# Modulation rows of a DiT layer: two alternating accumulators, one product with ones per step, plain stores, biases added behind

## The reference, cut to what matters

```python
mod_x = (jax.nn.silu(c) @ w_mod[l] + b_mod[l])[:, None, :]        # 1024 -> 6 * 1024
mod_c = (jax.nn.silu(c_ctx) @ w_mod[l] + b_mod[l])[None, None, :]
sh1, sc1, g1, sh2, sc2, g2 = jnp.split(mod_x, N_MOD, axis=-1)
...
hx = modulate(x, norm_mix_g[l], sh1, sc1)      # rms_norm(x) * (1 + scale) + shift
hc = modulate(ctx, norm_mix_g[l], csh1, csc1)
fx, qx, kx, vx = split_projection(hx @ w_in[l])     # 1024 -> 1536
fc, qc, kc, vc = split_projection(hc @ w_in[l])
...                                             # q, k normed per head, rotary; attention; Fourier mix
x = x + g1 * (jnp.concatenate([four_x, attn_x], axis=-1) @ w_out[l])
x = x + g2 * expert_choice_ffn(modulate(x, norm_ffn_g[l], sh2, sc2), ...)   # 16 experts
```

## Time and profile before

| | |
|---|---|
| median of 3 runs | 2109.92 us (2108.83 to 2115.02) |
| profiled execution, its own time | 2115.79 us |
| its span, first to last instruction | 2114.0 us |
| TensorE busy | 1878.2 us, 89% |
| DVE busy | 1604.0 us, 76% |
| ACT busy | 1305.0 us, 62% |
| POOL busy | 267.5 us, 13% |
| mean granted TensorE clock | 0.95 |

### The profile page before, as it was taken

The page is one execution under the profiler, slowest core; times in us unless marked ns, Lnnn a source line. Parts: engine busy times, 40 slices in busy tenths (PEclk is TensorE's granted clock), DMA queues, the critical chain, the costliest instruction groups (busy, mean ns, idle before and its releaser), DMA issues.

```text
span 2114.0 us, 28075 instructions
## 1 busy us (share of the span) xinstructions
PE 1878.2 (89%) x8737; PEld 1469.3 (70%) x8737; DVE 1604.0 (76%) x2017; ACT 1305.0 (62%) x1930; POOL 267.5 (13%) x303
## 2 busy tenths in 40 slices
PE   6889758988998998843999999999999999999993
PEld 2667545666666666623888888888888888888882
DVE  1576745686767667637988989998988889998983
ACT  2634215675667656622777777777777777777772
POOL 0133211121111111100111001100111001100111
PEclk9989878999999999976999999999999999999996
DMA  8255437021011101024999999999999999999985
GB/s 340 87 138 155 119 85 183 19 61 60 20 40 60 42 27 50 30 110 154 413 392 378 380 400 388 376 381 388 401 378 384 374 401 385 377 375 392 393 314 196
DMA packets 103747, 509.69 MB, mean 241 GB/s; under 512 B 12504, under 2 KB 36496, under 8 KB 53008
## 3 DMA queue, kind: packets, MB, share of 16 engines
q1 hardware_dynamic: 95264, 482.55, 60.4%
q0 software_dynamic: 5120, 16.80, 3.3%
q10 hardware_dynamic: 3312, 9.70, 1.2%
HBM read 479.11 MB, written 27.30 MB: 240 GB/s over the span
## 4 chain that ended last, share of the span: by engine, by line
PE 50%; issue 2%; DVE 2%; DMA 1%; ACT 0%; POOL 0%; ACTq 0%; POOLq 0%; SPq 0%
PE banks L1476 32%; PE banks L1501 16%; PE banks L1488 1%; PE banks L1457 1%; DVE topi L1347 1%; DVE top L1345 1%; DVE cand L1348 1%; DMA xe<-h_scratch,icol 0%; DMA acc_scratch<-ysc,idx_s 0%; DVE raw L1440 0%; ACT raw L1334 0%; DMA raw<-acc_scratch 0%; POOL fst L1261 0%; POOL fst L1263 0%; POOL gate_s L1244 0%
## 5 line engine op out<-in xcount | busy, mean ns | idle before, releaser
L1379 DVE TENSOR_TENSOR w_lo<-raw,w_hi 128x2048 fp32r<-128x2048 f32 x256 | 574.6, 2285 | 67.8 <-ACT w_hi L1283 67.8
L1283 ACT ACTIVATE w_hi<-raw 128x2048 fp32r<-128x2048 f32 x256 | 470.5, 1919 | 8.5 <-DMA raw<-in_w_exp 8.5
L1476 PE MATMUL banks<-w_hi,x_hi 128*128 128x512 f32 x1024 | 405.5, 396 | 1.4 <-DVE x_lo L1373 1.4
L1476 PE MATMUL banks<-w_hi,x_lo 128*128 128x512 f32 x1024 | 400.1, 391 | 0.0
L1476 PE MATMUL banks<-w_lo,x_hi 128*128 128x512 f32 x1024 | 399.5, 390 | 0.0
L1387 DVE TENSOR_TENSOR d_lo<-raw,d_hi 128x1024 fp32r<-128x1024 f32 x256 | 296.1, 1216 | 1.5 <-ACT d_hi L1305 1.4
L1305 ACT ACTIVATE d_hi<-raw 128x1024 fp32r<-128x1024 f32 x256 | 258.3, 1061 | 35.8 <-DMA raw<-in_w_exp 21.1
L1476 PEld LDWEIGHTS banks<-w_hi,x_lo 128*128 128x128 f32 x1024 | 192.7, 188 | 40.8
L1476 PEld LDWEIGHTS banks<-w_hi,x_hi 128*128 128x128 f32 x1024 | 193.0, 189 | 39.8 <-DVE x_lo L1373 1.8
L1476 PEld LDWEIGHTS banks<-w_lo,x_hi 128*128 128x128 f32 x1024 | 193.1, 189 | 38.2
L977 DVE TENSOR_TENSOR ptl<-banks,pth 128x384 fp32r<-128x384 f32 x320 | 176.3, 554 | 55.7 <-ACT pth L923 51.4
(11 more groups left out here) (195 smaller groups left out, 2781.8 us busy)
## 6 DMA issues: line engine op xcount, KB each, us to landing
raw<-in_w_exp SPq DMA_DIRECT2D x384, 1024.0 KB, 7.8
a_ring<-in_w_mod SPq DMA_DIRECT2D x32, 512.0 KB, 4.4
qt<-q_scratch SPq DMA_DIRECT2D x64, 192.0 KB, 3.5
a_slot<-in_w_mod SPq DMA_DIRECT2D x8, 1024.0 KB, 13.7
a_w_raw<-in_w_in SPq DMA_DIRECT2D x3, 2048.0 KB, 27.5
q_scratch<-a_qst SPq DMA_DIRECT2D x16, 384.0 KB, 3.9
a_xt<-in_x ACTq DMA_DIRECT2D x8, 512.0 KB, 3.7
xr<-in_x SPq DMA_DIRECT2D x8, 512.0 KB, 4.2
```

What stands on the lines that cost most here:

```text
L1283: act.activation(w_hi[which][c][:, :], raw[which][c][:, :], ACT.Copy).then_inc(s["hi_done"], 1)
L1379: dve.tensor_tensor(w_lo[which][c][:, :], raw[which][c][:, :], w_hi[which][c][:, :].bitcast(F32), ALU.subtract).then_inc(s["lo_done"], 1)
L1476: i = pe.matmul(psum[:, 2 * (j % 2) + which, :], x_[par][:, k, :], w_, start=(k == 0 and w_ is hi and x_ is x_hi), stop=(k == KD - 1 and x ...
```

## The change

1. The accumulator is one tile of 128 x 2 x 256. A step's two units advance together: DVE's instructions alternate between the two halves of the tile, first the lower halves of both units (`modulation(n, 0)`, ahead of `sums`), then the upper halves (`modulation(n, 1)`, between `sums` and `rotate`). Each waits for the one before it on its own half, thus two back, in place of a wait after each instruction. Nothing stands between `rotate` and `low` any more.
2. One product with ones per step, of 512 columns, behind `project(n, 2)`. ACT copies it to a row `mrow` of its own ahead of the next `normal`; SP stores it plainly ahead of `store`. POOL has no DMA left in phase A. The accumulator is free when the product has been made (`row_mm`).
3. The ring's order: a step's four halves are now (unit 0 low, unit 1 low), (unit 0 high, unit 1 high).
4. The biases are added in phase B: SP loads four more vectors of `b_mod` (512 KB each as spread) behind `rows` and ahead of `x2`, and POOL adds them in four instructions of 128 x 1024 ahead of the two that make `rows[SC2]`.
5. Prologue: ACT rounds chunk 2 of `w_in` only behind the last `c_rows` copy; tile 1 of x is loaded earlier; chunks 1 and 0 are rounded at other places; the square of a tile is written to PSUM, not to SBUF. `ON_DVE` is empty, so all of the first eight units stay on TensorE and `first_unit` is not called.

```diff
-            sp.dma_start(mod_d, a["b_mod"][0][2 * D:6 * D]).then_inc(s["preset"], 16)
...
+            def row_store(n):
+                sp.wait_ge(s["row_ev"], n + 1)
+                sp.dma_start(mod_d[n * 2 * UM:(n + 1) * 2 * UM].unsqueeze(0), mrow[:, :]).then_inc(s["row_out"], 16)
...
-                for i in range(2 * units[0], 2 * units[0] + 3) if units else ():
-                    load(i)
+                for i in range(3) if TC <= n < TS else ():
+                    load(4 * (n - TC) + i)
+                if TC < n <= TS:
+                    row_store(n - 1 - TC)
                 if n >= 2:
                     store(n - 2)
-                if units:
-                    load(2 * units[0] + 3)
+                if TC <= n < TS:
+                    load(4 * (n - TC) + 3)
...
-            def row_out(u):
...
-                pool.dma_start(mod_d[u * UM:(u + 1) * UM].unsqueeze(0), acc[u % 2][0:1, :], accum_op=ALU.add).then_inc(row_out_done[u % 2], 16)
...
-                if u >= NC_UNITS - 2:
-                    weights(2, u - NC_UNITS + 2)
+                if i == 1:
+                    load_x(1)
+            weights(2, 0)
+            weights(2, 1)
...
+            def modulation(n, half):
+                i0 = 4 * n + 2 * half
+                last = [(s["mod_used"], i0 - 1), (s["mod_used"], i0)] if half else [None, None]
                 if half == 0:
-                    after(dve, row_out_done[u % 2], 16 * (u // 2))
+                    after(dve, s["row_mm"], n)
                 for k in range(4):
+                    for x in range(2):
+                        slot_ = (i0 + x) % RING
+                        if k == 0:
+                            dve.wait_ge(ring_in[slot_], 16 * ((i0 + x) // RING + 1))
+                        ins = weigh(acc[:, x, :], ring[slot_][:, k * UM:(k + 1) * UM], c_sig[:, 4 * half + k, 0:1], last[x], half == 0 and k == 0)
...
-                pe.matmul(psum[0:1, MB, 0:UM], ones[:, 0:1], acc[u % 2][:, :], start=True, stop=True).then_inc(s["row_mm"], 1)
+                pe.matmul(psum[0:1, MB, :], ones[:, 0:1], acc[:, :, :].rearrange("p a n -> p (a n)"), start=True, stop=True).then_inc(s["row_mm"], 1)
...
-            sp.dma_start(x2[:, :], a["norm_ffn_g"][0].partition_broadcast(P)).then_inc(s["rows_in"], 16)
+            for dst, v in ((h2[:, :], a["b_mod"][0][2 * D:3 * D]), (junk2[:, :], a["b_mod"][0][3 * D:4 * D]), (h2t[:, :, :].rearrange("p k n -> p (k n)"), a["b_mod"][0][4 * D:5 * D]),
+                           (xr[:, :], a["b_mod"][0][5 * D:6 * D]), (x2[:, :], a["norm_ffn_g"][0])):
+                sp.dma_start(dst, v.partition_broadcast(P)).then_inc(s["rows_in"], 16)
...
-            pool.wait_ge(s["rows_in"], 32)
+            pool.wait_ge(s["rows_in"], 16 * 6)
+            for i, tmp in ((G1, h2[:, :]), (SH2, junk2[:, :]), (SC2, h2t[:, :, :].rearrange("p k n -> p (k n)")), (G2, xr[:, :])):
+                pool.tensor_tensor(rows[:, i, :], rows[:, i, :], tmp, ALU.add).then_inc(s["bias_done"], 1)
```

More of the change, by code:

```diff
@@ L203, in w_parts @@
         return 2 * (2, 1, 0).index(c)
-    def units_of(n):
-        return (2 * (n - TC), 2 * (n - TC) + 1) if lat(n) else ()
+    ON_DVE = ()
+    ON_PE = tuple(u for u in range(NC_UNITS) if u not in ON_DVE)
     with nc.Block() as block:
@@ new lines, in first_unit @@
+            def first_unit(i, u):
+                last = [None, None]
+                dve.wait_ge(unit_in[u], 16)
+                for k in range(KD):
+                    for j in range(2):
+                        ins = weigh(first_acc[i][:, j, :], slot[u][:, k, :], c_sig[:, k, j:j + 1], last[j], k == 0)
+                        if k == KD - 1 and j == 1:
+                            ins.then_inc(s["first_used"], 1)
+                        else:
+                            order[0] += 1
+                            ins.then_inc(s["dve_order"], 1)
+                            last[j] = (s["dve_order"], order[0])
```

180 lines of the change are left out of this document (93 added, 87 removed).

## The result

The changed kernel takes 2095.7 us (median of 4 runs, 2094.6 to 2099.4) against 2111.2 us (2108.8 to 2115.0) of the kernel before, run beside it: 15.5 us less, ratio 0.9928, 95% interval 0.9908 to 0.9948. Measured a second time beside later experiments it was 2095.4 us, ratio 0.9932 (0.9911 to 0.9952). The forecast was 16.5 us less.

The account below looks back on a forecast made before the run. DVE's chain of work and waits was taken to bound the latent steps, TensorE following. Phase A -28.5 and phase B +12 make -16.5 us, forecast 2093 us; the range leaving out 2 in 10 is 2083 to 2107.

Parts of the forecast that it names:

- The wait: Phase A: DVE's wait for the accumulating DMA, 42.7 us in 7 waits, holds up the latent steps and would go.
- The step, 20.7 us: Latent step's DVE chain: ring landed 11.6, seven instructions 2.8, rotary 4.98, `low` 1.27; 20.7 us against 25.6 before.
- The clock in the steps: Latent steps: TensorE's wait stays under a microsecond, so its clock holds.
- TensorE alone, 20.0 us: Phase A step if only TensorE bound it: 17.8 us, plus one wide product and the transposes of `queries`.
- The alternation, 0.40 an instruction: DVE's modulation: an alternating instruction takes 0.40 us, where linked ones take 0.51; at 0.51, 4 us of gain go.
- The prologue, +2.0: Before the first projection: chunk 2's second rounding starts 1.9 us later, and the first projection with it, +2.0 us.
- Phase A, -28.5 in all: Step 9 begins at 223.5 against 252.04, so phase A takes 28.5 us less.
- Phase B, +12: Start of phase B: transfer 7.9 and additions 9.6 against 6.7 of slack, plus 1.2 of slow clock: +12 us.
- The lock: Rival, phase A: POOL's square starts before `low`, each step 1.7 us longer, about 13 us in all, 2106; chance 0.17.
- slower mechanism: Rival, phase A: ring load late, each microsecond beyond 4.4 going into some 6 steps; chance 0.12, half of it above 2104.
- The kernel with hidden biases: Rival: loads land at 3.5 us and phase B loses only 6, 9 us better, 2084; chance 0.10.
- A landing at 8.5 us: Case of a late ring load in phase A: at 8.5 us the kernel is 7 us slower, 2118.

Follow-up runs that it names:

- experiment 4: Kernel before the change with four accumulators and four DMA semaphores in place of two, ACT's square written to PSUM: 2082.8 us, 0.9872.
- three edits and queries: Changed kernel with fourth ring half loaded between stores, chunk 2's roundings earlier, biases added inside tile 0, ACT's queries ahead of normalization: 2074.7 us, 0.9836.
- four accumulators and queries: Kernel before the change with four accumulators in place of two and ACT's queries copied ahead of its normalization: 2074.1 us, 0.9823.
- the linked kernel: Changed kernel with DVE waiting for the end of each modulation instruction before the next: 2097.0 us, 0.9930.
- experiment 6: Changed kernel with chunk 2's two roundings on ACT put back between the last c_rows copies: 2092.1 us, 0.9916.
- experiments 1, 2: Changed kernel without phase B's bias loads and additions: 2088.3 us, 0.9886; with the loads but without the additions: 2086.5 us, 0.9884.
- experiment 7: Changed kernel with POOL's bias additions moved inside tile 0 of phase B, behind the first diag: 2085.8 us, 0.9883.
- experiment 5: Changed kernel with the load of the step's fourth ring half issued between the q and k stores, not behind them: 2090.8 us, 0.9904.

## Why the prediction was right, step by step

**The wait.** Right, and shown: removing it alone (experiment 4) gives 27 us and the same step as the whole change. One reading was wrong: the DMA that POOL issues behind the power, at 135.02, is not that of unit 0. DVE's instruction at 137.17 begins unit 1 in the second accumulator, and waits for the DMA of unit 1 of the step before; unit 0's went out at 142.23. That the power holds DVE up is true all the same: ACT had copied that row by 132.81, and the DMA went out only when the power had ended.

**The step, 20.7 us.** 21.43 and 20.77 in two executions. In the step shown each link behind the first store held: ring load 5.7 us behind it, landed after 4.3, seven instructions in 2.78, rotary 4.98, `low` 1.2. The first link did not. The store came 3.2 us into the step (123.55 against 120.34) and not 1.5, since DVE had waited 1.76 us for ACT's `queries`, and the step took 22.3 us. The next step had no such wait, the store came 1.6 us into it, and the rotary began after 14.15 us where the sum has 14.4. The sum had this term only once, with 0.6; in this trace it is 1.76, 1.59, 0.80 and 1.13 us in four of the seven rows from 122 us on, and nothing in the other three. Moving ACT's copies took a third to a half of all such waits away and moved the time by 2 us, not told from nothing, so how much of the 0.1 to 0.7 that the step is over comes from this term stays open.

**The clock in the steps.** The sentence that TensorE's wait stays under a microsecond was wrong for four waits (2.60, 2.26, 2.06 and 1.94 us), and with it that the clock holds. Behind the waits of 2.60 and 2.06 us the granted clock was at half first, behind that of 2.26 it was not. The two steps that began at half took 21.19 and 21.22 us from transposes to transposes without a wait: there TensorE was the bound after all. In the second execution the waits in the steps were 0.59 to 1.85 us, the clock was full behind each, and the same two steps took 20.24 and 20.33. That is 1.9 of the 4.0 us by which the two executions differ over six steps.

**TensorE alone, 20.0 us.** Too high by 0.7. Two windows of whole steps, from transposes to transposes, without a wait and at full clock: the first with one wide product (three edits and queries), the second with two narrow ones (four accumulators and queries), where the same count gives 21.2:

```profile
115.74:135.05 19.31, 19.31 (x91) 15.13 (x90) 16.37 (x29) 7.83 (x16) 6.14 (x4) 1.00 0.63 176
...
135.83:155.59 19.76, 19.76 (x93) 15.29 (x92) 17.29 (x28) 9.60 (x21) 9.19 (x8) 1.00 0.69 186
```

Records of neighbours overlap, and I had added their full lengths. A unit's product holds the engine for 0.52 us and not 0.59, and in the kernel with three edits and queries the wide product holds it for 0.95 (134.10 to 135.05) and not the 1.2 I allowed, the transposes of the queries for 0.85 (135.05 to 135.90) and not 1.03. That makes 19.0 - 1.04 + 0.95 + 0.85 = 19.8; the other 0.45 us down to 19.31 these records do not explain. In the forecast the bound did not count, since the chain was longer; it made my expectation for the last experiment wrong.

**The alternation, 0.40 an instruction.** Right as a duration. As a term it stays open: I had charged 4 us if it were 0.51, and at 0.50 the time did not move beyond its uncertainty, while the steps of the linked kernel make some 3 us.

**The prologue, +2.0.** Right for the first projection: 52.34 for 50.37; experiment 6 takes it back. Behind it something was missed. Step 2 begins 3.3 us later than before (80.44 against 77.10; 2.9 in the second execution), and step 3 at 101.06 and 100.22 where the sum had 99.4. What I had costed at nothing, the other roundings and the earlier load, lies in that stretch; no run separates it. TensorE, which took 19.3 us and not 20.0 for step 3, gave 0.7 us of it back.

**Phase A, -28.5 in all.** Phase B starts 26.1 us earlier in the one execution and 30.7 in the other, against a single trace of the kernel before.

**Phase B, +12.** The mechanism right, the size 8.5 to 9.6 by the stretch of tile 0 (7.7 to 9.8 over the six traces with the additions ahead), and 9 to 10 by experiments 1, 2 and 7. The term that was mis-sized is the transfer of 7.9 us, worked out with the 267 GB/s of the earlier trace rows as if the queue were full; it was 4.6 us. A DMA share of 0.95 in that row did not mean that the rate was at its limit: in the changed kernel ten slices with the broadcasts in them run at 311 to 419 GB/s. The additions (forecast 9.6, measured 9.4) and the slack of 6.7 held: 14.0 - 6.7 = 7.3, and TensorE waited 7.47. The slow clock, on the other hand, I had priced at 1.2 us, and some 2 us are left for it. The Trainium skill (SBUF — State Buffer, section The DMA setup-cost knee) had put the transfer, as an estimate, at 4.8 us and phase B at +9, which is what the trace shows; its 3.2 us for a ring half was again too short, the median being 4.8.

**The rivals.** The lock did not come: `low` was 1.22 or 1.23 us long in all seven steps, and it was POOL's square that grew, to 2.74 in three. The order of the two was not forced the other way in any run. POOL's power of 2.92 us ended inside DVE's wait for the ring (132.22 against 133.58), so what it would do to the alternating instructions is not seen. No slower mechanism showed: the ring loads on the chain of the six steps from 120.34 on landed 4.1 to 5.5 us after their issue, and the longest of all, 9.3, was not among them. The kernel with hidden biases, forecast as a rival at 2084, exists as experiment 7, at 2085.8.

That the total came so near, 15.5 for 16.5, is partly luck, two errors that cancel: by the times phase A gave 4 us less than its term (15.5 and the 9 of phase B make 24.5), and phase B took 3 less. In the profiled pair the two are 2.4 each (26.1 and 9.6), which makes 16.5, and the span is 16.4 shorter.

**Small slips.** The plain product at 137.17 is 0.35 us long and not 0.34. A landing at 8.5 us would by its own sum be 8 us slower, as the 2118 beside it says, and not 7. The profiled execution's own time is 1.8 above its span and not 1.7. None moves the forecast.

## What to carry to other kernels

Before a wait is restructured away, try the smallest thing that lengthens its cycle. Two more buffers of 1 KB gave 27 us where a redesign around two gave 15, and 9 of the 12 us between them went because the redesign moved the biases into a place with 6.7 us of slack. Ask of each added instruction not how long it is but what stands behind it in its queue at the first use: four additions cost 9 us ahead of the first `diag` and nothing behind it. And a saving of 0.1 us on each of many instructions counts only for those behind the last wait of the chain: here seven of a step's sixteen, too little for the times to show. And before a step's bound is added up from record lengths, look for a step in which the engine never waits, and read its length.

## What was unexpected of the hardware

A power on POOL of one element per partition took 0.55 us with DVE idle or reading one input from PSUM, 1.46 beside DVE's rotary and 1.41 beside `low`, and POOL's square 1.89 and 2.74: in the changed kernel POOL was the one that slowed, and DVE's instructions of 128x1024 with two inputs kept 1.22 to 1.23 us. In the kernel before one row went the other way, `low` at 2.92 us behind a square that had begun 0.05 us earlier. SP's issuing, not a transfer, set when the ring load could start: 1.06 us for each strided k store and 0.62 for each q store, 5.5 us for a step's six, against 0.33 for the ring's load of 512 KB in experiment 5. A wait of 2.60 us left TensorE at half its clock for over 3 us though it was busy in all of them, and one of 7.47 us for over 5; one of 2.06 us was followed by half the clock too, and one of 2.26 in the same trace was not.
